# Another order of the first instructions in a two-layer encoder trunk on one core

## What is computed

```python
for l in range(2):
    h = rms_norm(x, norm_mix); z = h @ w_in          # w_in: 1024 x 6340
    za, bq, bk, bv, cq, clat, ciq, cik, ciw, zd, zg = split(z)
    ya = gmlp_mixer(gelu(za)); yb = swa_sink_mixer(bq, bk, bv)
    yc = dsa_mixer(cq, clat, ciq, cik, ciw); yd = pool_mixer(zd)
    gates = sigmoid(zg)                              # four of them, 256 x 1024 each
    merged = sum(g * (y @ w_out) for g, y in zip(gates, (ya, yb, yc, yd)))
    x = x + merged @ w_o
    gate, up = split(rms_norm(x, norm_ffn) @ w_gate_up)
    x = x + (silu(gate) * up) @ w_down               # FFN_HIDDEN 2816
```

## Time and profile before

| | us |
|---|---|
| median of 3 runs (843.8 to 844.58) | 844.17 |
| the profiled execution | 844.2 |
| its span in the trace | 842.5 |
| outside the span | 1.7 |
| PE busy | 816.5 (97%) |
| DVE busy | 572.3 (68%) |
| ACT busy | 408.9 (49%) |

### The profile page before, as it was taken

The page is one execution under the profiler, slowest core; times in us unless marked ns, Lnnn a source line. Parts: engine busy times, 40 slices in busy tenths (PEclk is TensorE's granted clock), DMA queues, the critical chain, the costliest instruction groups (busy, mean ns, idle before and its releaser), DMA issues.

```text
span 842.5 us, 10195 instructions
## 1 busy us (share of the span) xinstructions
PE 816.5 (97%) x3876; PEld 664.3 (79%) x3876; DVE 572.3 (68%) x858; ACT 408.9 (49%) x557; POOL 45.1 (5%) x84
## 2 busy tenths in 40 slices
PE   4999999999999999999999999999999999999998
PEld 3888777778778888888888876777878888888886
DVE  8799588893766565456568968888755865456543
ACT  5756555553354443444366644656443643344330
POOL 6230000000000000000005100000000000000000
PEclk9999999999999999999999999999999999999999
DMA  7735435465265656566663535266454566565641
GB/s 216 275 103 179 148 110 200 142 198 186 69 214 186 210 188 198 153 212 189 190 208 122 188 113 176 75 200 197 151 174 148 180 206 194 159 210 187 193 150 50
DMA packets 99072, 144.25 MB, mean 171 GB/s; under 512 B 11728, under 2 KB 62416, under 8 KB 99024
## 3 DMA queue, kind: packets, MB, share of 16 engines
q1 hardware_dynamic: 99024, 143.60, 52.8%
HBM read 142.54 MB, written 1.05 MB: 170 GB/s over the span
## 4 chain that ended last, share of the span: by engine, by line
PE 81%; DVE 8%; DMA 4%; ACT 3%; issue 3%; SPq 0%; DVEq 0%; ACTq 0%
PE big L1391 16%; PE big L1395 16%; PE big L1394 16%; PE mix L1395 9%; PE mix L1394 9%; PE mix L1391 9%; DMA w_raw<-in_w_in 3%; DVE w_lo L961 3%; DMA w_raw<-in_w_gate_up 1%; ACT w_hi L624 1%; PE mix L1684 1%; PE mix L1441 1%; PE mix L1469 1%; PE mix L1454 1%; PE mix L1417 1%
## 5 line engine op out<-in xcount | busy, mean ns | idle before, releaser
L624 ACT ACTIVATE w_hi<-w_raw 128x2048 fp32r<-128x2048 f32 (+2 forms) x140 | 256.4, 1835 | 172.3 <-DMA w_raw<-in_w_gate_up 111.0
L961 DVE TENSOR_TENSOR w_lo<-w_raw,w_hi 128x2048 fp32r<-128x2048 f32 (+3 forms) x139 | 301.1, 2182 | 32.1 <-ACT w_hi L624 31.7
L1391 PE MATMUL big<-w_hi,act_hi 128*128 128x512 f32 (+2 forms) x480 | 189.4, 395 | 12.8 <-DVE act_lo L978 6.2
L1394 PE MATMUL big<-w_lo,act_hi 128*128 128x512 f32 (+2 forms) x480 | 184.5, 384 | 0.0
L1395 PE MATMUL big<-w_hi,act_lo 128*128 128x512 f32 (+2 forms) x480 | 184.4, 384 | 0.0
L1391 PE MATMUL mix<-w_hi,act_hi 128*128 128x512 f32 x352 | 137.5, 391 | 0.8 <-issue 0.8
L1395 PE MATMUL mix<-w_hi,act_lo 128*128 128x512 f32 x352 | 137.2, 390 | 0.0
L1394 PE MATMUL mix<-w_lo,act_hi 128*128 128x512 f32 x352 | 137.0, 389 | 0.0
L1391 PEld LDWEIGHTS big<-w_hi,act_hi 128*128 128x128 f32 x480 | 91.2, 190 | 36.7 <-issue 9.0
L1395 PEld LDWEIGHTS big<-w_hi,act_lo 128*128 128x128 f32 x480 | 91.1, 190 | 17.6
L1196 DVE TENSOR_TENSOR y_h_lo<-mix,y_h_hi 128x256 fp32r<-128x256 f32 x44 | 16.6, 420 | 129.9 <-ACT y_h_hi L829 129.9
(11 more groups left out here) (189 smaller groups left out, 728.5 us busy)
## 6 DMA issues: line engine op xcount, KB each, us to landing
w_raw<-in_w_in SPq DMA_DIRECT2D x44, 1024.0 KB, 5.1
w_raw<-in_w_gate_up SPq DMA_DIRECT2D x88, 512.0 KB, 4.7
w_raw<-in_w_down SPq DMA_DIRECT2D x22, 1024.0 KB, 4.9
w_raw<-in_w_o SPq DMA_DIRECT2D x8, 1024.0 KB, 4.9
w_raw<-in_b_w_out SPq DMA_DIRECT2D x4, 1024.0 KB, 5.2
w_raw<-in_w_in SPq DMA_DIRECT2D x4, 904.0 KB, 6.2
w_raw<-in_w_in SPq DMA_DIRECT2D x4, 512.0 KB, 3.6
w_raw<-in_a_w_out SPq DMA_DIRECT2D x4, 512.0 KB, 4.0
```

The costliest lines, as they stand in the source:

```text
L624: nc.scalar.activation(high(u), arrived(u), ACT.Copy).then_inc(hi_ready.sem, 1)
L961: nc.vector.tensor_tensor(low(u)[:, a:], arrived(u)[:, a:], high(u)[:, a:].bitcast(F32), ALU.subtract).then_inc(lo_by_dve, 1)
L1391: ins = nc.tensor.matmul(dst[:, 0:w], xh, wh, start=first and n == 0, stop=False)
L1394: nc.tensor.matmul(dst[:, 0:w], xh, wl, start=False, stop=False)
```

## The change

- **Transfers.** Block 0 of the tokens, the gain, the first two pieces of unit 0, block 1 of the tokens, the other two pieces, unit 1, unit 2, and only then the small parameters.
- **Splits by half units.** Units 0 and 1 are split in halves of two pieces, by ACT and DVE alone; POOL has no part in it any more. The gain steps of both blocks stand between them. `first_segment` lets PE begin with high x high of two pieces, as their parts appear.
- **Constants behind the first sums.** The last steps of the angles stand on DVE behind the split of unit 1, sine, cosine and both table fetches on ACT in slot 0 behind the split of unit 2 and the squares of x, and the eight subtractions for the averages (lines 941, 943) in slot 11. The waits for the parameters stand in slot 2 on DVE and in slot 3 on PE.
- **Products of zeros.** DVE clears `rope_t` first, and PE multiplies it with itself four times before it turns the tokens.

The core of the diff:

```diff
         def _(sp):
-            for tb in range(TB):
+            def load_tokens(tb):
                 sp.dma_start(xs[:, tb], x[0, tok(tb)]).then_inc(x_in[tb], 16)
...
+                if (l, u) == (0, 0):
+                    for half, k in ((0, slice(0, 2)), (1, slice(2, 4))):
+                        sp.dma_start(dst[:, k, 0:b], ...).then_inc(first_in if half == 0 else landed[s].sem, 16)
+                        if half == 0:
+                            load_tokens(1)
...
+            load_tokens(0)
+            load_gain(0)
             for l in range(DEPTH):
-                if l == 0:
-                    load_gain(0)
                 load_unit(l, 0)
                 load_unit(l, 1)
-                load_params(l)
+                if l > 0:
+                    load_params(l)
                 for u in range(2, NU):
                     load_unit(l, u)
+                    if l == 0 and u == 2:
+                        load_params(0)
...
         def _(pool):
-                if l == 0:
-                    split_first(0, 0, 2)
-                    split_first(0, 2, 4)
-                    split_first(SHARED, 0, 2)
...
         def _(act):
-                    nc.scalar.activation(act_spare[:], minus_half[:, 0:1], ACT.Exp).then_inc(alone_act, 1)
-                    split(0, 0)
+                    split(0, 0, 0)
                     high_gained(0, "hT", 0)
-                    split(0, 1)
-                    high_gained(0, "hT", 1)
-                    x_squares(0, "mix", 0)
-                    x_squares(0, "mix", 1)
+                    split(0, 0, 1)
+                    high_gained(0, "hT", 1, [0])
+                    split(0, 1, 0)
+                    high_gained(0, "hT", 1, [1])
+                    split(0, 1, 1)
                 for s in range(SLOTS):
...
                         split(*ahead)
+                    if (l, s) == (0, 0):
+                        x_squares(0, "mix", 0)
+                        x_squares(0, "mix", 1)
+                        tables()
...
         def _(dve):
+            nc.vector.memset(rope_t[:], 0.0).then_inc(warm_in, 1)
...
-                    gained(0, "hT", 0)
-                    gained(0, "hT", 1)
-                    split(0, SHARED)
-                mean_of_sums(l, "mix", D_MODEL)
-                dve.wait_ge(*params_in.nth(l, params_in.per_layer))
+                    gain_half(0, "hT", 0, 0)
+                    gain_half(0, "hT", 0, 1)
+                    split(0, 0, 0)
+                    gain_low(0, "hT", 0, 0)
+                    gain_half(0, "hT", 1, 0)
+                    split(0, 0, 1)
+                    gain_low(0, "hT", 1, 0)
+                    gain_low(0, "hT", 0, 1)
+                    gain_half(0, "hT", 1, 1)
+                    split(0, 1, 0)
+                    gain_low(0, "hT", 1, 1)
+                    split(0, 1, 1)
+                    angles_reduced()
+                else:
+                    mean_of_sums(l, "mix", D_MODEL)
...
+                    if (l, s) == (0, 0):
+                        mean_of_sums(0, "mix", D_MODEL)
+                        tables_completed()
+                    if (l, s) == (0, 11):
+                        averages_centred()
...
         def _(pe):
+            def first_segment():
+                for half, a, b in halves_of(0, 0):
+                    pe.wait_ge(*high_part(0, 0, half))
+                    pe.wait_ge(*act_hi_ready.nth(0, 1))
+                    # high x high of pieces a to b
+                    pe.wait_ge(*low_part(0, 0, half))
+                    # high x low of pieces a to b
+                    pe.wait_ge(*gained_low(0, "hT", 0, 0))
+                    # low x high of pieces a to b
...
+            pe.wait_ge(warm_in, 1)
+            zeros = rope_t[:].rearrange("p h d -> p (h d)")
+            for _ in range(4):
+                nc.tensor.matmul(big[:, 3, 0:SEQ], zeros[:, 0:P], zeros[:, 0:SEQ], start=True, stop=True)
```

More of the change, by code:

```diff
@@ L97 @@
 SLOTS = SLOT[-1] + 1
-SHARED = 1
-FIRST_BY_DVE = list(range(SHARED, NU))
+HALVED = 2
 def dmas_of(unit):
@@ L914, in _ @@
             dve.wait_ge(const_dve, done + 2)
-            done += 2
-            at = angle.rearrange("p t k -> p (t k)").unsqueeze(1).to_broadcast([P, len(TURNS), TB * HD // 2])
-            flat = [b.rearrange("p a t k -> p a (t k)") for b in (turns, reduced)]
-            for part in TWO_PI:
-                nc.vector.scalar_tensor_tensor(out=flat[1], in0=flat[0], scalar=-part, in1=at,
-                                               op0=ALU.mult, op1=ALU.add).then_inc(const_dve, 1)
-                done += 1
-                dve.wait_ge(const_dve, done)
-                at = flat[1]
@@ L924, in _, with angles_reduced @@
[L924 to L927 removed]
+            def angles_reduced():
+                done = 8 + len(TURNS) + 2
+                at = angle.rearrange("p t k -> p (t k)").unsqueeze(1).to_broadcast([P, len(TURNS), TB * HD // 2])
+                flat = [b.rearrange("p a t k -> p a (t k)") for b in (turns, reduced)]
+                for part in TWO_PI:
+                    nc.vector.scalar_tensor_tensor(out=flat[1], in0=flat[0], scalar=-part, in1=at,
+                                                   op0=ALU.mult, op1=ALU.add).then_inc(const_dve, 1)
```

163 lines of the change are left out of this document (98 added, 65 removed).

## The result

The changed kernel took **850.86 us** in the median of 4 runs (848.34 to 852.04), the kernel before 844.09 (843.8 to 844.58) beside it: 1.0067 times, 95% interval 1.005 to 1.0084. It is slower, where 845.3 and no measurable change were predicted, and above the range. The profiled execution is the quickest of the four, 848.34 with a span of 846.6; the other three show a mean granted clock of 0.986 to 0.990 instead of its 0.992. Before: 844.2, span 842.5, clock 0.998. So the trace accounts for 4.1 of the 6.8 us.

What follows compares the result with a forecast made beforehand. PE, busy 816.5 of 842.5 us, was taken as the bound, with unit 3's landing deciding. 844.2 + 0.8 (unit 3 start -1.1, clock +1.9) + 0.3 (averages) = 845.3 us, range 842.3 to 846.8.

Steps and rivals of the forecast that it cites:

- What bounds the kernel: Whole kernel: PE busy 816.5 of 842.5 us; up to slot 10 PE and DVE hang on unit 3's landing.
- The start: Beginning of the kernel: unit 0's first half lands at about 7.5, PE ends the four `idx` segments 5.5 us earlier.
- Unit 3's landing: Transfers behind the parameters: unit 3 issued at 18.0, landing 6.7 later at 24.7 against 24.9 us before.
- The gap: PE after its first `kv` half: stands 4.4 us, then starts unit 3 at 29.0 instead of 30.1, -1.1 us.
- The clock: PE behind its wait for unit 3: lower clock for 3.4 to 5.1 us, costing 1.9 (1.7 to 2.5).
- (a): Rival: the clock holds after PE's gap at unit 3; 844.1 us, chance 0.17.
- The averages: Slot 12: the averages, moved behind unit 13's split on DVE, are ready at 86.0 and cost PE +0.3 us.
- The zero products: PE before the tokens land: hidden, cost nothing, and give at most a faster turning.
- (c): Rival: the queue holds the parameters longer, unit 3 lands at 26.2; 846.8 us (846.1 to 847.5), chance 0.17.
- (b): Rival: the queue does not hold the parameters, unit 3 lands by 23; 842.2 to 843.5 us, chance 0.18.
- (d): Rival: the change does what it says, PE keeps all 5.5 us; 838.7 us, chance 0.03.

Runs made afterwards that it cites:

- e10: Changed kernel with layer 0's parameters issued by ScalarE on its own queue, ahead of its first split: 853.78 us, 1.0086 of the kernel before.
- e12: Changed kernel with layer 0's fourteen parameters issued in three lots, behind units 2, 3 and 4: 845.19 us, 0.9993 of the kernel before.
- e15: Changed kernel with units 2 to 5 of layer 0 also split by halves: 849.12 us, 1.0053 of the kernel before.
- e18: Kernel before the change, with layer 0's parameters spread in three lots behind units 2, 3 and 4: 846.53 us, 1.0034 of the kernel before.
- e16: e12 without the products of zeros and with the averages centred in slot 0 again: 844.20 us, 0.9995 of the kernel before.
- e8: Changed kernel without the four products of zeros ahead of the transposes: 849.01 us, 1.0042 of the kernel before.
- e4: Changed kernel with 32 useless identity products on PE ahead of unit 3's first product: 845.89 us, 1.0002 of the kernel before.
- e3: Changed kernel with the fourteen parameters issued behind unit 4 instead of behind unit 2: 845.71 us, 0.9999 of the kernel before.
- e5: Changed kernel with layer 0's parameters issued behind unit 3 instead of behind unit 2: 849.24 us, 1.0047 of the kernel before.
- e17: e16 with 12 extra identity products on PE in the gap before unit 3: 843.23 us, 0.9979 of the kernel before.

## Why the prediction was wrong, point by point

- **What bounds the kernel: right.** An earlier TensorE is worth what the next thing allows; 5 us of earlier sums gave nothing. Unit 3 was the term that decides.
- **The start: right.** First half at 7.43 (7.5), first sum 9.55 (10.7; the other traces of this beginning but e10 have 10.2 to 11.7), `g_lat` released at 11.67 (11.5), unit 3 issued at 17.85 (18.0). The queue did hold SyncE, 5.55 us.
- **Unit 3's landing: the step that failed.** "Unit 3 is now the first: 18.0 + 6.7" measured 17.85 + 9.2. I had moved the issue with the queue's filling but carried the time from issue to landing over as a constant. The runs show that it isn't one: 6.7 behind two units and the parameters, 7.7 to 9.6 behind three or more. I also read the stretch of the parameters as packets to be worked off, so that "what must be through before unit 3 is the same"; e12 shows it as a hole that small transfers in a row leave and large ones between them mostly fill.
- **The gap** followed: 7.4 for 4.4, PE at unit 3 +1.3 for -1.1, a difference of 2.4, which is the 2.3 of the landing.
- **The clock: right in kind, small in size.** 1.9 forecast, between 1.7 and 2.5; measured 3.88 - 1.31 = 2.6, since it stayed low for 5.9 us. The rule of the Trainium skill ("TensorE: Matmul & The Clock Gate", on HAM oscillation), a wait for a transfer and then the half clock, agrees with the 0.43 between products from 31.39 to 37.3, and again in e15 behind 5.5 us. Behind shorter gaps the runs go both ways (e12 and e18). Without the term the prediction's sum is 844.1, as its rival (a) has it, and not 844.0.
- **The averages: right.** 0.35 waited at `pool_b`, +0.4 in the difference; 0.3 had been counted; e16 removes it.
- **The zero products: right as far as shown.** "At most a faster turning" is what the traces have (0.11 for 0.21), and no slower first sums go with them (e8).
- **Layer 1: missing.** +1.6 between 90 and 492 us against before, 1.2 of it a longer wait for DVE at unit 11 again, and 2.2 back by the end, 1.7 of it where before has its own low clock at 522. Beyond the trace, the medians hold 2.7 more, in runs with a lower mean clock; no step spoke of that, and its cause stays open.
- **The rivals.** (c) comes nearest: unit 3 late, a longer gap, the low clock behind it. But its reason is not what was measured, since SyncE was held as forecast and unit 3 was issued on time; the time from there to the landing was longer. It put the landing at 26.2 and the time at 846.8. With 27.0 and the measured clock its own sum is 844.2 + 1.3 + 2.6 + 0.3 = 848.4, beside the profiled execution's 848.34. That close agreement is partly luck: at the averages the difference is 4.6 where the sum has 4.2, and the two differences in layer 1 nearly cancel. The median, 850.86, lies above even (c)'s 847.5. (b) is refuted by the 5.55, (d) by the landing at 27.0, (a) by the 0.43.

## What to carry to other kernels

Fourteen small transfers in a row left a hole of some 7 us in one queue here, about as long as their issues; put large ones between them, and check first that no engine waits for all of them at once. Where an engine is brought forward, ask whose chain is next and how much play it has: here unit 3's landing, then the tables, then VectorE up to 73 us, each of which took the whole gain by itself. And a gap in TensorE's work costs its length and often the slow products behind it, so a start that is early and interrupted can be worse than a late one that runs through.

## What the runs showed of the hardware that I had not expected

- The same transfer took 6.7 us from issue to landing behind two units and the parameters, and 7.7 to 9.6 behind three or more units and the parameters. With the very same issues ahead it was 7.7 in one trace (e8) and 9.6 in another (e4).
- A gap of 2.0 us (e3) and one of 2.8 (e12) brought the low clock as one of 7.4 did; for 5.9 us behind 7.4, for 3.7 behind 2.8. But gaps of 2.8 (e18, at 30.1) and 3.0 (e5, at 76.5) did not. Useless products in the gap kept it high (e4, e17).
- In the first 12 to 20 us of some traces the granted clock reads 1.00 while the products go at half pace (before up to 19.8, e16 up to 14.7). There the starts have to be read.
- GpSimd's and ScalarE's queues moved the parameters beside the units, but the last one landed 10.3 and 15.7 after its issue, where it was 4.3 in before and 6.1 in after, and ScalarE was held at issuing until 14.5 us.
